# Key and value rows of the compression stored by offset within the stride, so that 66 moving elements lie in a row

## The chip, the cores and the metric

The kernel runs on one core of a Trainium2 chip. The metric is the device time of one execution in microseconds, as the median of several runs. The core has five engines with queues of their own: TensorE (PE in the profile, and PEld for its weight loads), VectorE (DVE), ScalarE (ACT), GpSimd (POOL) and SyncE (SP), which here only issues transfers.

## What is computed

Two transformer blocks over 512 tokens of width 1024, all in 32-bit floats. The change lies in the first block, in the compression of keys and values (`compress`): from the raw key (or value) rows of 512 tokens, 2 groups of 64 elements each, it takes overlapping windows of 32 tokens at a stride of 16, adds a position term, and sends each window of 32 x 64 = 2048 numbers through a small two-layer network.

```python
CMP_LEN, CMP_STRIDE, CMP_HIDDEN = 32, 16, 256

def compress(kv_raw, pos, w1, w2):
    B, T = kv_raw.shape[0], kv_raw.shape[1]
    nc = (T - CMP_LEN) // CMP_STRIDE + 1
    idx = jnp.arange(nc)[:, None] * CMP_STRIDE + jnp.arange(CMP_LEN)[None, :]
    blocks = kv_raw[:, idx] + pos[None, None, :, None, :]
    blocks = blocks.transpose(0, 1, 3, 2, 4).reshape(B, nc, N_KV_GROUPS, CMP_LEN * HEAD_DIM)
    return jax.nn.gelu(blocks @ w1) @ w2
...
    kc = rms_norm(compress(kv_heads(kcr), cmp_pos_k, cmp_w1_k, cmp_w2_k), k_cmp_norm_g)
    vc = compress(kv_heads(vcr), cmp_pos_v, cmp_w1_v, cmp_w2_v)
```

Everything else (the input projection, the three attention branches, the state-space mixer, and the whole second block) is the same before and after.

## The kernel before

Each engine runs one instruction stream that is written out by hand; the order on an engine is the order of the code, and semaphores (`S[...]`) tie the streams together. The 128 partitions hold a contraction index, the free axis holds tokens or columns. Large matrices are streamed from memory in "chunks" through a ring of two slots (`slot(c)`); SP issues the load of chunk c once TensorE has counted up `w_free` for the chunk two before it.

The part of the first block around the change runs on TensorE in this order.

1. Projections of the input: `proj_T` for the state-space input (4 tiles), then for the raw keys and the raw values (PT_KC and PT_KC + 1), each leaving a 128 x 512 result in a PSUM bank: partitions are 2 groups x 64 elements, columns are tokens. `proj_tok` follows for further keys and values (PT_KV, PT_KW). A projection tile may start once ScalarE has emptied the bank three or four tiles back (`proj_evac`).
2. ScalarE copies the raw keys (s = 0) and raw values (s = 1) into `x2`, a view of the buffer `xn_t` (lines 681 to 686). For each group g it writes the 512 tokens to the lower 64 partitions (line 684), and the same row moved by one token to the upper 64 partitions (line 685). So one column holds tokens t and t + 1, and one product contracts over two tokens x 64 elements = 128. GpSimd has zeroed the tail of each row before and put the position terms there as two extra windows (lines 522 to 526, counted by `zeroed`).
3. Transposes (L1122), the small products that build a Toeplitz kernel from the state-space weights (16 output columns), and the products behind `v_done`, 64 of them, each with 64 stationary columns and 64 moving elements.
4. The query projection, `proj_tok(PT_Q, ...)`.
5. **The compression's first layer**, lines 1152 to 1173. For s = 0, 1 (keys, values), for each half of the window (part), each half m of the 256 hidden units, each of 8 pairs of tokens lp, and each half h of 64 hidden units, one product: stationary 128 x 64 weights, moving 66 elements of `x2` (32 windows of group 0, 2 position columns, 32 windows of group 1). That is 2 x 2 x 2 x 8 x 2 = 128 products. The two products of h write the lower and the upper 64 partitions of one bank and read the same moving elements. The moving elements stand `CS` = 16 numbers, 64 bytes, apart:

```python
at_ = 2 * (KD * part + lp)
flat[:, at_:at_ + 65 * CS + 1:CS]
```

The key weights are chunk 6 (`ring`); the first half of the value weights lies in `arena` (`w1v_first`, loaded from ScalarE's queue at L717), the second half is chunk 7 (`w1v_last`), for which TensorE waits at s = 1, part = 1. After each s, TensorE counts `hid_done` and `w_free` up; the latter lets SP load chunk 8, then chunk 9 (the weights of the two gate projections).
6. The output of the state-space mixer, counted by `y_done`: 128 products with 64 stationary columns and 64 contiguous moving elements; again two neighbouring products fill the two halves of a bank and read the same moving elements (`toe_of(g)` and `cl3` against `u_in` and `st`).
7. `proj_T` for the gate projection (PT_ZS), with the compression's second layer inside its third tile; it needs `hid_gelu` from VectorE, which adds the positions and computes the gelu (L1893 to L1913) with ScalarE's tanh (L724) in between.

The later use of `xn_t` (line 731 on) is for other data.

Of the kernel before, what the change touches and what calls it, by code (L numbers as in the profile page):

```python
# [9 lines left out]
T = 512  # L10
D = 1024
P = 128
NT = T // P
KD = D // P
AW = 512
NH, HD, NG = 8, 64, 2
CL, CS, NCMP = 32, 16, 32
SG, SC, SN = 32, 16, 64
GP = SG // 2
LC = 8  # L20
NCH = T // LC
NAH, DAH, DAV = 8, 4, 128
GRID, GROWS = 64, 8
# [39 lines left out]
def build(nc, io):  # L63
# [3 lines left out]
    ACT = mybir.ActivationFunctionType  # L67
# [4 lines left out]
    with ctx:  # L72
# [9 lines left out]
        def cut(view, **dims):  # L82
            return view.rearrange("p (" + " ".join(dims) + ") -> p " + " ".join(dims), **dims)
# [7 lines left out]
        xn_t = sb("xn_t", 2 * NG * (T + 2 * CS))  # L91
# [46 lines left out]
        bank = [ctx.enter_context(nc.psum_tensor(f"bank{i}", [P, 512], fp32)) for i in range(8)]  # L138
# [4 lines left out]
        def col(name):  # L143
            return cols[:, COLS[name][0]:COLS[name][1]]
# [7 lines left out]
        x = cut(x_t[:, :], i=NT, f=D)  # L152
        hT = cut(hT_t[:, :], k=KD, t=T)
        xn = cut(xn_t[:, 0:2 * D], b=2, f=D)
        x2 = cut(xn_t[:, :], s=2, g=NG, t=T + 2 * CS)
        prob = cut(soft[:, 0:4 * T], b=4, t=T)
        probT = cut(soft[:, 4 * T:6 * T], b=2, t=T)
        ident = con("ident")
# [341 lines left out]
        @block.gpsimd  # L500
        def _(pool):
            steps = [0]

            def settle(ins):
                ins.then_inc(S["pool_step"], 1)
                steps[0] += 1
                pool.wait_ge(S["pool_step"], steps[0])

            def inv_root(mean, eps, done, of):

                settle(pool.tensor_scalar(of(ss), of(ss), 1.0 / mean, eps, MUL, ADD))
                pool.tensor_tensor(of(rstd), of(ss), of(mhalf), ALU.pow).then_inc(S[done], 1)

            def by_tile(v):
                return cut(v[:, 0:48], i=NT, h=12)

            settle(pool.memset(mhalf, -0.5))
            settle(pool.memset(gate_b[:, :], 0.0))
            pool.wait_ge(S["x_stats"], 1)
            inv_root(D, EPS, "x_rstd", lambda v: v[:, 0:NT])  # L520
            pool.wait_ge(S["xT_done"], 2 * NT)
            settle(pool.memset(x2[:, :, :, T - 1:T + 2 * CS], 0.0))

            pool.wait_ge(S["params_in"], 32)
            settle(pool.tensor_copy(x2[:, 0, 0, T:T + 2 * CS:2], col("pos_k")))
            pool.tensor_copy(x2[:, 1, 0, T:T + 2 * CS:2], col("pos_v")).then_inc(S["zeroed"], 1)
            pool.wait_ge(S["cl_ready"], 1)
            settle(pool.memset(soft[:, 0:2048], 0.0))
            pool.wait_ge(S["cl_ready"], 2)
            pool.memset(spent, 0.0).then_inc(S["zeroed"], 1)  # L530
            pool.wait_ge(S["k_stats"], 1)
            inv_root(HD, EPS, "k_rstd", lambda v: by_tile(v)[:, :, 8:12])
            for r in range(2):
                pool.wait_ge(S["q_stats"], r + 1)
                inv_root(HD, EPS, "q_rstd", lambda v: by_tile(v)[:, 2 * r:2 * r + 2, 0:8])
            pool.wait_ge(S["k_stats"], 2)
            inv_root(HD, EPS, "k_rstd", lambda v: v[0:NG * NCMP, 48:49])
            pool.wait_ge(S["proj_done"], PT_ZA + 4)
            for i in range(NT):
                pool.dma_start(x[:, i, :], io["x"].rearrange("(r c) f -> c r f", r=GROWS)[16 * i:16 * (i + 1)]).then_inc(S["x_back"], 16)  # L540

            pool.wait_ge(S["ssm_ready"], 4)
            for f in range(4, KD):
                settle(pool.tensor_copy(a_hi[:, f, :], hT[:, f, :]))
                pool.tensor_tensor(hT_r[:, f, :], hT[:, f, :], a_hi[:, f, :].bitcast(fp32), SUB).then_inc(S["ssm_lo"], 1)
            pool.wait_ge(arrive[CH_WO % SLOTS], landed(CH_WO))
            for j in range(4):
                pool.tensor_copy(wo_hi(j), wo_raw(0, j)).then_inc(S["wo_hi"], 1)
                pool.wait_ge(S["wo_hi"], j + 1)
                pool.tensor_tensor(wo_lo(0, j), wo_raw(0, j), wo_hi(j).bitcast(fp32), SUB).then_inc(S["wo_lo"], 1)  # L550

            def load_bias(n):
                l, h = divmod(n, LOADS)
                if n >= 2:
                    pool.wait_ge(*bias_read(n - 2))
                if h < DAH:
                    pool.dma_start(bias_ring[:, n % 2, 0:896], io["t5_bias"][h]).then_inc(bias_in[n % 2], 16)
                else:
                    src = io["na_bias"][l, 2 * (h - DAH):2 * (h - DAH) + 2].rearrange("h p j -> p h j")
                    pool.dma_start(cut(bias_ring[:, n % 2], h=2, j=1024), src).then_inc(bias_in[n % 2], 16)  # L560

            def x_rstd(r):

                sums = cut(ssq[:, 0:2 * NT], c=2, i=NT)
                for a in range(2):
                    pair = slice(2 * a, 2 * a + 2)
                    pool.wait_ge(S["n_stats"], 2 * r + a + 1)
                    settle(pool.tensor_tensor(ss[:, pair], sums[:, 0, pair], sums[:, 1, pair], ADD))
                    inv_root(D, EPS, "n_rstd", lambda v: v[:, pair])

            pool.wait_ge(S["x_ready"], 1)
            for l in range(LAYERS + 1):
                if l:
                    pool.wait_ge(S["xn_ready"], NT * (l + 1))
                pool.dma_start(gain, io["gains"][l]).then_inc(S["gain_in"], 16)
                x_rstd(l)
                if l == LAYERS:
                    break
                at_ = LOADS * l
                for n in range(at_ + (2 if l else 0), at_ + DAH + 2):  # L580
                    load_bias(n)
                pool.wait_ge(S["o_stats"], l + 1)
                inv_root(DAV, SUB_EPS, "o_rstd", lambda v: v[:, 0:NT * DAH])
                for n in range(at_ + DAH + 2, min(at_ + LOADS + 2, LOADS * LAYERS)):
                    load_bias(n)
# [3 lines left out]
        def _(act):  # L589
# [15 lines left out]
            for i in range(NT):  # L605

                ins = act.activation(xn[:, i % 2, :], x[:, i, :], ACT.Square, accum_out=ss[:, i:i + 1])
# [67 lines left out]
            for f in range(4):  # L675
                src = proj(PT_U + f)[:, :].rearrange("p (n s) -> p s n", s=LC)
# [4 lines left out]
            for s in range(2):  # L681
                src = proj(PT_KC + s)
                for g in range(NG):
                    act.activation(x2[0:HD, s, g, 0:T], src[g * HD:(g + 1) * HD, :], ACT.Copy)
                    ins = act.activation(x2[HD:P, s, g, 0:T - 1], src[g * HD:(g + 1) * HD, 1:T], ACT.Copy)
                ins.then_inc(S["proj_evac"], 1)
                part_hi(8 + s)
            part_hi(10)
# [6 lines left out]
            for i in range(NT):  # L695
                src = proj(PT_KV + i)
# [7 lines left out]
            for i in range(NT):  # L704
                src = proj(PT_KW + i)
# [12 lines left out]
            for i in range(NT):  # L718
                src = proj(PT_Q + i)
# [45 lines left out]
            for i in range(NT):  # L765
# [3 lines left out]
                if i == 0:  # L769
                    act.wait_ge(S["kc_T"], 1)  # L770
                    for u in range(2):
                        half_ = slice(u * HD, (u + 1) * HD)
                        ins = act.activation(kcT[half_, :, u, :], cut(bank[7][half_, 0:NG * NCMP], g=NG, j=NCMP), ACT.Copy)
# [167 lines left out]
            for l in range(LAYERS):  # L941
                for half in (1, 0):
                    for g in range(4 - 4 * half, 8 - 4 * half):
                        for t in range(4):
                            u = first_unit(l, g + 1)
# [52 lines left out]
        def _(pe):  # L998
# [3 lines left out]
            def mm(out, lhsT, rhs, first, last):  # L1002
                return pe.matmul(out, lhsT, rhs, start=first, stop=last)  # L1003
# [146 lines left out]
            w1k = slot(CH_W1, 16, 256)  # L1150
            w1v_last = slot(CH_W1 + 1, KD, 256)
            for s in range(2):
                flat = x2[:, s].rearrange("p g t -> p (g t)")
                for part in range(2):
                    if s and part == 0:
                        pe.wait_ge(S["w1v_in"], 16)
                    elif part == s:
                        arrived(CH_W1 + s)
                    w = (w1v_last if part else w1v_first) if s else w1k[:, KD * part:KD * (part + 1)]
                    for m in range(2):  # L1160
                        if s == 0 and part == 0:
                            pe.wait_ge(S["proj_evac"], PT_Q + 3 + m)
                        for lp in range(KD):
                            at_ = 2 * (KD * part + lp)
                            for h in range(2):
                                c = m * P + h * SN
                                ins = mm(bank[m][h * SN:(h + 1) * SN, s * 66:(s + 1) * 66], w[:, lp, c:c + SN], flat[:, at_:at_ + 65 * CS + 1:CS],
                                         part == 0 and lp == 0, part == 1 and lp == KD - 1)
                ins.then_inc(S["hid_done"], 1)
                pe.wait_ge(S["hid_done"], s + 1)  # L1170
                pe.sem_inc(S["w_free"], 1)
# [82 lines left out]
            w = slot(CH_GLU, 4, 512)  # L1254
# [1097 lines left out]
```

## Time and profile before

| | us |
|---|---|
| Time before, median of 3 runs | 973.33 (971.76 to 974.12) |
| The profiled execution's own time | 974.55 |
| its span, first to last instruction | 972.7 |
| TensorE busy in it | 925.0 (95%) |
| VectorE busy | 579.5 (60%) |
| ScalarE busy | 453.5 (47%) |
| GpSimd busy | 66.6 (7%) |

The span is what the trace covers; the profiled execution's time holds 1.85 us more, outside of it. "took" or "mean ns of one" is the time from start to modelled end of one instruction. Matmuls overlap, so the price of one in a dense row is the distance from start to start, and not what it took. A 32-bit product stands in the trace as two matmul records and two weight-load records: the 128 products of the compression are 256 records of each kind. "issue" is time in which an engine waited for nothing that the profile shows.

### The profile page before, as it was taken

The numbers are of one execution on the slowest core, as the hardware profiler recorded it, in microseconds if no ns is written. First come the engines' busy times: TensorE is split into PE (matmuls) and PEld (weight loads), VectorE is DVE, ScalarE is ACT, GpSimd is POOL, SyncE is SP. The second block draws the span as 40 slices with busy tenths as digits, with TensorE's granted clock in tenths as the row PEclk, the third lists the DMA queues.
The fourth block names the chain that finished last, engine by engine and source line by source line (L and its number), as shares of the span: only waits on it lengthen the run. The fifth ranks groups of instructions, "written<-read, shape, count | busy, mean of one in ns | idle before, by whom it ended". The sixth has DMA issues, their size and how long they took to land.

```text
span 972.7 us, 14853 instructions
## 1 busy us (share of the span) xinstructions
PE 925.0 (95%) x5845; PEld 725.6 (75%) x5845; DVE 579.5 (60%) x1177; ACT 453.5 (47%) x974; POOL 66.6 (7%) x82
## 2 busy tenths in 40 slices
PE   3999999999999999999999989999999999998995
PEld 1689897764667788886788867888886778886784
DVE  5899867977886472438762347254244964435632
ACT  4635124455785343336824248233423853426730
POOL 1001120004400010000010000000000010000000
PEclk9999999999999999998999999999999899998999
DMA  9845654265100333432304323132443123323102
GB/s 357 311 115 130 149 174 140 98 174 193 68 2 3 106 125 87 119 98 62 107 25 127 108 89 105 42 93 80 111 131 103 45 84 108 87 94 102 66 1 87
DMA packets 94807, 104.71 MB, mean 108 GB/s; under 512 B 15953, under 2 KB 65105, under 8 KB 94738
## 3 DMA queue, kind: packets, MB, share of 16 engines
q1 hardware_dynamic: 89586, 86.62, 29.1%
q0 software_dynamic: 3824, 15.73, 5.1%
q10 hardware_dynamic: 1328, 1.41, 0.5%
q8 instruction: 47, 0.77, 0.3%
q14 instruction: 22, 0.18, 0.1%
HBM read 98.37 MB, written 4.19 MB: 105 GB/s over the span
## 4 chain that ended last, share of the span: by engine, by line
PE 83%; DVE 6%; ACT 5%; issue 3%; DMA 3%; DVEq 0%; SPq 0%; POOL 0%; POOLq 0%; ACTq 0%; PEldq 0%
PE bank L1003 77%; DVE ring L2016 2%; PE bank L1332 2%; ACT ring L913 2%; DMA ring<-in_w_in 2%; PE bank L1312 1%; DMA ring<-in_w_ada 1%; PE bank L1470 1%; ACT soft L920 1%; PE bank L1388 1%; ACT w_hi L863 0%; PE bank L1378 0%; ACT hT_hi L845 0%; DVE small L1596 0%; ACT arena L710 0%
## 5 line engine op out<-in xcount | busy, mean ns | idle before, releaser
L2071 DVE TENSOR_TENSOR w_lo<-ring,w_hi 128x1024 fp32r<-128x1024 f32 x80 | 97.7, 1225 | 114.7 <-ACT w_hi L863 111.9
L1003 PE MATMUL bank<-w_hi,hT_hi 128*128 128x512 f32 x320 | 125.3, 392 | 1.3 <-issue 1.0
L1003 PE MATMUL bank<-hT_hi,w_hi 128*128 128x512 f32 x320 | 125.7, 393 | 0.0
L1003 PE MATMUL bank<-w_lo,hT_hi 128*128 128x512 f32 x320 | 124.6, 389 | 0.0
L1003 PE MATMUL bank<-hT_lo,w_hi 128*128 128x512 f32 x320 | 124.6, 389 | 0.0
L1003 PE MATMUL bank<-w_hi,hT_lo 128*128 128x512 f32 x320 | 124.6, 389 | 0.0
L1003 PE MATMUL bank<-hT_hi,w_lo 128*128 128x512 f32 x320 | 124.5, 389 | 0.0
L863 ACT ACTIVATE w_hi<-ring 128x1024 fp32r<-128x1024 f32 x80 | 84.4, 1058 | 11.7 <-PE bank L1003 11.4
L1003 PEld LDWEIGHTS bank<-w_hi,hT_hi 128*128 128x128 f32 x320 | 60.1, 188 | 14.8 <-issue 2.6
L1003 PEld LDWEIGHTS bank<-hT_hi,w_hi 128*128 128x128 f32 x320 | 60.1, 188 | 13.1 <-issue 0.7
L1003 PEld LDWEIGHTS bank<-hT_lo,w_hi 128*128 128x128 f32 x320 | 60.1, 188 | 12.7
L1003 PEld LDWEIGHTS bank<-w_lo,hT_hi 128*128 128x128 f32 x320 | 60.1, 188 | 12.6
L1003 PEld LDWEIGHTS bank<-w_hi,hT_lo 128*128 128x128 f32 x320 | 60.1, 188 | 12.2
L1003 PEld LDWEIGHTS bank<-hT_hi,w_lo 128*128 128x128 f32 x320 | 60.1, 188 | 12.0
L868 ACT ACTIVATE bank<-x_t 128x512 f32<-128x512 f32 x24 | 14.5, 602 | 96.7 <-DVE x_t L2267 63.4
L1003 PE MATMUL bank<-arena 128*64 128x64 f32 (+5 forms) x608 | 51.0, 293 | 2.1 <-issue 1.7
L815 ACT ACTIVATE ring<-ring,small 128x512 f32<-128x512 f32 x64 | 45.7, 715 | 15.5 <-DVE small L2016 12.7
L2203 DVE SCALAR_TENSOR_TENSOR k_lo<-bank,k_hi 128x512 fp32r<-128x512 f32 x16 | 11.1, 692 | 53.2 <-ACT k_hi L933 53.2
L1003 PEld LDWEIGHTS bank<-arena 128*64 128x64 f32 (+1 forms) x608 | 31.1, 147 | 14.4 <-issue 12.6
L2016 DVE CUSTOM_DVE_ANT_0 ring<-bank,bias_ring 128x512 f32<-128x512 f32 x64 | 41.4, 684 | 0.0
L913 ACT ACTIVATE ring<-ring,small 128x256 f32<-128x256 f32 x64 | 31.9, 499 | 14.4 <-DVE small L2149 14.2
L2267 DVE TENSOR_TENSOR x_t<-bank,x_t 128x512 f32<-128x512 f32 x16 | 11.0, 689 | 45.9 <-PE bank L1003 45.9
(312 smaller groups left out, 1811.1 us busy)
## 6 DMA issues: line engine op xcount, KB each, us to landing
ring<-in_w_in SPq DMA_DIRECT2D x66, 512.0 KB, 4.5
ring<-in_w_ada SPq DMA_DIRECT2D x4, 2048.0 KB, 14.1
ring<-in_w_in SPq DMA_DIRECT2D x4, 2048.0 KB, 8.9
bias_ring<-in_na_bias POOLq DMA_DIRECT2D x8, 1024.0 KB, 5.6
ring<-in_w_out SPq DMA_DIRECT2D x16, 512.0 KB, 3.4
ring<-in_w_out SPq DMA_DIRECT2D x2, 2048.0 KB, 8.1
bias_ring<-in_t_bias POOLq DMA_DIRECT2D x8, 448.0 KB, 3.7
x_t<-in_x SPq DMA_DIRECT2D x4, 512.0 KB, 5.8
```

The lines of the kernel that those rows point to most:

```text
L815: act.activation(p, p, ACT.Exp, scale=-1.0, bias=negm[:, k % 8:k % 8 + 1], accum_out=ssum[:, k % 8:k % 8 + 1])\
L863: act.activation(w_hi[:, u % 4], raw_w[:, u % 4], ACT.Copy).then_inc(S["w_hi_ready"], 1)
L868: settle(act.activation(place[:, 0:n], x[:, i, c0:c0 + n], ACT.Square, accum_out=ssq[:, part * NT + i:part * NT + i + 1]))
L913: act.activation(p, p, ACT.Exp, scale=-1.0, bias=negm[:, k % 16:k % 16 + 1], accum_out=ssum[:, k % 16:k % 16 + 1])\
L920: act.activation(probT2[:, m % 4, :], bank[m % 2][:, :], ACT.Copy).then_inc(S["na_moved"], 1)
L1003: return pe.matmul(out, lhsT, rhs, start=first, stop=last)
L1312: ins = pe.transpose(bank[u % 2][:, b * P:(b + 1) * P], src[:, b * P:(b + 1) * P], ident)
L1332: ins = pe.transpose(bank[k % 2][:, b * P:(b + 1) * P], prob1_of(k)[:, b * P:(b + 1) * P], ident)
L2016: dve.tensor_tensor_reduce(prob_of(k)[:, 0:width], bank[S_BANKS[k % 4]][:, 0:width], bias, -scale, 3.0e38, ADD, MIN, negm[:, k % 8:k % 8 + ...
L2071: dve.tensor_tensor(w_lo[:, u % 4], raw_w[:, u % 4], w_hi[:, u % 4].bitcast(fp32), SUB).then_inc(S["w_split"], 1)
L2203: dve.scalar_tensor_tensor(lo_[:, t, :], bank[(pt2(l, g) + t) % 4][:, :], SCALE if isq else 1.0, hi_[:, t, :].bitcast(fp32), MUL, SUB).the ...
L2267: dve.tensor_tensor(xs, bank[6 + t % 2][:, :], xs, ADD).then_inc(S["x_ready"], 1)
```

## The change

The buffer `xn_t` is read through another view, `win_x`, with the axes s (keys, values), r (8), g (2), j (34). Token t = 16 j + 2 r + u of group g stands in the partitions of half u at (r, g, j): r and u are the token's offset within the stride of 16, j is the stride that it lies in. j = 32 and 33 hold the zeros and the position columns that stood behind the tokens before.

```diff
-        x2 = cut(xn_t[:, :], s=2, g=NG, t=T + 2 * CS)
+        win_x = cut(xn_t[:, 0:2 * 8 * NG * WIN], s=2, r=8, g=NG, j=WIN)
...
-            settle(pool.memset(x2[:, :, :, T - 1:T + 2 * CS], 0.0))
+            for s in range(2):
+                settle(pool.memset(win_x[:, s, :, :, NCMP:WIN], 0.0))
 
             pool.wait_ge(S["params_in"], 32)
-            settle(pool.tensor_copy(x2[:, 0, 0, T:T + 2 * CS:2], col("pos_k")))
-            pool.tensor_copy(x2[:, 1, 0, T:T + 2 * CS:2], col("pos_v")).then_inc(S["zeroed"], 1)
+            pos_at = [win_x[:, s, :, 0, NCMP:WIN].rearrange("p r j -> p j r") for s in range(2)]
+            settle(pool.tensor_copy(pos_at[0], cut(col("pos_k"), j=2, r=8)))
+            pool.tensor_copy(pos_at[1], cut(col("pos_v"), j=2, r=8)).then_inc(S["zeroed"], 1)
...
                 for g in range(NG):
-                    act.activation(x2[0:HD, s, g, 0:T], src[g * HD:(g + 1) * HD, :], ACT.Copy)
-                    ins = act.activation(x2[HD:P, s, g, 0:T - 1], src[g * HD:(g + 1) * HD, 1:T], ACT.Copy)
+                    pairs = src[g * HD:(g + 1) * HD, :].rearrange("p (j r u) -> p u r j", j=NCMP, r=8, u=2)
+                    for u in range(2):
+                        ins = act.activation(win_x[u * HD:(u + 1) * HD, s, :, g, 0:NCMP], pairs[:, u], ACT.Copy)
...
-                flat = x2[:, s].rearrange("p g t -> p (g t)")
+                wins = win_x[:, s].rearrange("p r g j -> p r (g j)")
...
-                            at_ = 2 * (KD * part + lp)
...
-                                ins = mm(bank[m][h * SN:(h + 1) * SN, s * 66:(s + 1) * 66], w[:, lp, c:c + SN], flat[:, at_:at_ + 65 * CS + 1:CS],
+                                ins = mm(bank[m][h * SN:(h + 1) * SN, s * 66:(s + 1) * 66], w[:, lp, c:c + SN], wins[:, lp, part:part + 66],
```

With `WIN = NCMP + 2` = 34. A product for the second half of the window (part = 1) reads the same row r, one element further on. ScalarE reads its bank in steps of 16 numbers and writes 8 rows of 32 numbers, and it writes each token once, to the half of its parity, where before it wrote each token to both halves. GpSimd zeroes 2 x 32 numbers per partition in two instructions, for 132 in one.

No instruction changes its place on any engine; TensorE, VectorE and SyncE have the same instructions in the same order. What differs is the form of twelve instructions on ScalarE and GpSimd. ScalarE, after the projections of the state-space input, before:

```order
L663 ACTIVATE a_hi<-ring 128x1024
L684 ACTIVATE xn_t<-bank 64x512
L685 ACTIVATE xn_t<-bank 64x511
L684 ACTIVATE xn_t<-bank 64x512
L685 ACTIVATE xn_t<-bank 64x511
L663 ACTIVATE a_hi<-ring 128x560
```

and after the change (lines are 3 or 4 further down), the same stretch with the second group, for the values:

```order
L666 ACTIVATE a_hi<-ring 128x1024
L689 ACTIVATE xn_t<-bank 64x8x32 x4
L666 ACTIVATE a_hi<-ring 128x560
L689 ACTIVATE xn_t<-bank 64x8x32 x4
L666 ACTIVATE a_hi<-ring 128x560 x2
```

The eight copies stand where they stood, and each moves 256 numbers per partition in place of 512 or 511.

## Rows read from the trace of the kernel before

**Rows 1.** The page: the chain that ended last, shares by engine and line.
```profile
PE 83%; DVE 6%; ACT 5%; issue 3%; DMA 3%; DVEq 0%; SPq 0%; POOL 0%; POOLq 0%; ACTq 0%; PEldq 0%
```
**Rows 2.** The chain, 126 to 176 us: start us, us, what.
```profile
126.41 7.72 PE bank L1003 x128
134.13 0.14 issue
134.27 7.68 PE bank L1003 x128
141.96 0.29 issue
142.24 6.17 PE bank L1003 x204
148.41 1.72 issue
150.13 25.25 PE bank L1003 x168
```
**Rows 3.** Timeline of TensorE: start us, us, engine, line, operation, out<-in, shapes, count.
```profile
99.88 3.95 PE L1003 MATMUL bank<-arena 128*64 128x64 f32 x128
...
142.38 0.32 PE L1003 MATMUL bank<-arena 128*64 128x64 f32 x4
...
148.10 0.32 PE L1003 MATMUL bank<-arena,gate_b 128*64 128x64 f32 x4
```
**Rows 4.** Groups by line and shape: count | busy us, mean ns | idle before.
```profile
L1003 PE MATMUL bank<-xn_t,ring 128*64 128x66 f32 x192 | 11.6, 295 | 0.3 <-PE bank L1003 0.3
L1003 PE MATMUL bank<-arena,soft 128*64 128x64 f32 x64 | 3.8, 223 | 0.3 <-PE bank L1003 0.3
```
**Rows 5.** Windows: stretch, us, busy (records) of PE, PEld, DVE, ACT, POOL; clock, DMA, GB/s.
```profile
126.40:142.00 15.60, 15.38 (x256) 14.92 (x256) 8.59 (x8) 1.83 (x3) 7.24 (x4) 1.00 0.63 204
142.20:148.40 6.20, 6.16 (x204) 6.06 (x204) 5.68 (x17) 2.31 (x3) 0.00 (x0) 1.00 0.89 300
```
**Rows 6.** Timeline of SyncE, and the issues by line: KB each, us to landing.
```profile
126.23 0.39 SPq L453 DMA_DIRECT2D ring<-in_cmp_w_v  x1
134.24 0.37 SPq L453 DMA_DIRECT2D ring<-in_w_in  x1
...
ring<-in_w_in SPq DMA_DIRECT2D x2, 2048.0 KB, 8.9
...
ring<-in_cmp_w_v SPq DMA_DIRECT2D x1, 1024.0 KB, 5.8
ring<-in_glu_w SPq DMA_DIRECT2D x1, 1024.0 KB, 8.0
```
**Rows 7.** Timeline of VectorE around the end of the compression.
```profile
134.12 1.22 DVE L1810 TENSOR_REDUCE small<-soft 128x16 f32<-128x1024 f32 x1
142.05 0.16 DVE L1893 COPY small<-bank 128x2 f32<-128x2 f32 x1 [6.71 <-PE bank L1003]
...
147.68 2.36 DVE L1620 TENSOR_TENSOR ring_lo<-ring,a_hi 128x1024 fp32r<-128x1024 f32 x2
```
**Rows 8.** Timeline of ScalarE: an emptied bank read in steps of 8, the copies, the tanh.
```profile
58.11 0.60 ACT L677 ACTIVATE arena<-bank 128x512 f32<-128x512 f32 x1 [4.04 <-PE bank L1003]
...
69.83 0.59 ACT L684 ACTIVATE xn_t<-bank 64x512 f32<-64x512 f32 x1 [2.42 <-PE bank L1003]
...
144.72 0.42 ACT L724 ACTIVATE pw<-pw 128x256 f32<-128x256 f32 x1 [16.46 <-DVE pw L1903]
145.04 1.99 ACT L663 ACTIVATE a_hi<-ring 128x1024 fp32r<-128x1024 f32 x2
```
**Rows 9.** The page: records of PE and PEld, and the instruction queue's packets and MB.
```profile
PE 925.0 (95%) x5845; PEld 725.6 (75%) x5845; DVE 579.5 (60%) x1177; ACT 453.5 (47%) x974; POOL 66.6 (7%) x82
...
q8 instruction: 47, 0.77, 0.3%
```
**Rows 10.** Timeline of TensorE in the token projection behind the raw values.
```profile
69.63 0.28 PE L1003 MATMUL bank<-a_hi,x_hi 128*128 128x256 f32 x1
69.87 0.28 PE L1003 MATMUL bank<-ring_lo,x_hi 128*128 128x256 f32 x1
69.98 0.28 PE L1003 MATMUL bank<-a_hi,x_hi 128*128 128x256 f32 x1
```
**Rows 11.** Timeline of GpSimd, the last of the instructions that the change touches there.
```profile
26.65 0.66 POOL L526 COPY xn_t<-cols 128x16 f32<-128x16 f32 x1
```

More of the change, by code:

```diff
@@ L20 @@
 LC = 8
+WIN = NCMP + 2
 NCH = T // LC
```

## The prediction, made before the changed kernel ran

> **What bounds the kernel now.** I read the shares of the chain of waits first: TensorE holds 83% of it [rows 1], so what counts is time on TensorE's own stream, and time saved on another engine counts only where TensorE waits for it. Then I read the chain in the stretch of the change. From 126.41 to 141.96 us it is nothing but the compression's 256 matmul records, two pieces of 7.72 and 7.68 us, and behind them the mixer's output in two pieces with a hole of 1.72 us between, and the gate projection [rows 2]. No other engine stands in it. So the compression is on the path with its full length, 7.72 + 7.68 = 15.40 us.
>
> Then the price of one record. 15.40 us / 256 = **60.2 ns** from start to start for 66 moving elements. The same kind of record with 64 contiguous moving elements is to be had twice. In the mixer's output, fours of records start 142.38 ... 148.10 us, 49 fours apart, so 5.72 / 196 = **29.2 ns**; in the products behind `v_done` it is 3.95 us for 128, at most 30.9 ns with the tail of the last one in it [rows 3]. Shapes, weights (64 stationary columns), the change of halves within a bank and the granted clock (1.00, the 2.4 GHz level, in both stretches [rows 5]) are the same. Neither is it only the distance: a record took 295 ns in the compression and 223 ns in the mixer's output [rows 4], 72 ns more, so each streams for longer. The weight loads follow the matmuls in both (256 and 204 of each [rows 5]), and they run at 29.2 ns there, so they are not what holds the compression at 60. What is left is the one thing that differs: 66 elements 64 bytes apart against 64 in a row, at twice the price.
>
> No row shows 66 contiguous elements, or strided ones elsewhere. The Trainium skill (SBUF — State Buffer, section Specifications (TRN2)) says that SBUF is read in lines of 16 bytes and that each step to a new line pays a penalty; it gives no amount. By it, and this is an estimate from the page's figure, every one of the 66 reads pays now, and about one in four would after.
>
> **The change, part by part.**
>
> *The 128 products.* Contiguous, a record should cost 29.2 x 66/64 = 30.1 ns, the whole 256 x 30.1 = 7.71 us, so **15.40 - 7.71 = 7.7 us less**. By the other stretch's 30.9 ns it is 256 x 31.9 = 8.2 us, so 7.2 us less. I take 7.7, since 30.9 holds a tail. The other bound is that the stride was innocent: 0.
>
> *ScalarE's eight copies.* They are 0.59 us each now [rows 8]. A bank read in steps of 8 numbers took 0.60 for 512 elements [rows 8], the same as these contiguous ones, so steps cost ScalarE nothing there; with 256 elements each is between 0.3 (half) and 0.6 us. Nobody waits for them: the values' copies begin at 69.83 us and the first reader of their semaphore on TensorE is the fourth token tile of the next projection. The records there start 0.117 us apart (69.63, two later 69.87, 69.98) [rows 10], 12 per tile, so the fourth starts 36 x 0.117 = 4.2 us behind 69.63, at 73.8; the copies end at 72.3 now. Saved time there is idle time: 0.
>
> *GpSimd.* One more small instruction; the last of these ends at 27.3 us [rows 11], and ScalarE asks for it at 64.3. Hidden by 37 us: 0. At the next bound, 0.66 us each as the dearest copy, still 0.
>
> *What follows the compression earlier.* Four things have to be there 7.7 us sooner, or 3.9 us for those halfway.
> First `w1v_last`: issued at 126.23, 5.8 us to landing [rows 6], so there at 132.0. It is wanted after three quarters of the compression: 138.03 now, then 126.41 + 0.75 x 7.71 + 0.14 = **132.3**. It just fits, with 0.3 us to spare. Another load of the same size took 8.0 us [rows 6]; by that it lands at 134.2 and TensorE waits 1.9 us. I take 0, since 5.8 is this load's own time and nothing else is queued ahead of it, and keep 1.9 for the range.
> Second the gate weights: issued when s = 0 is done, 134.24 now, then 126.41 + 3.86 + 0.1 = 130.4; 8.9 us to landing [rows 6] is 139.3. ScalarE's split follows the tanh, 144.72 now [rows 8]. VectorE sits idle for 6.71 us before the compression's end and is done with its squares at 134.12 + 1.22 = 135.34 [rows 7]; with the compression done at 134.3 it can start at 135.4 in place of 142.05, 6.65 us earlier and no more. So tanh at 138.1, split of the first tile at 139.3 to 140.4, and VectorE's low parts, whose pair ends at 147.68 + 2.36 = 150.04 now [rows 7], at 143.4 to 143.5. TensorE wants the gate projection's first tile at 151.8 - 7.7 = 144.1. All three fit, the closest by 0.6 us.
> Third `hid_gelu`, wanted 17 us into the gate projection: far. Fourth SP's own queue: it waits for TensorE's counts and comes earlier with them.
>
> *The hole of 1.72 us.* It is put down to "issue": TensorE waited for nothing that the profile shows, in the middle of one run of products [rows 2]. The candidate is the supply of instructions. Queue 8 moved 47 packets, 0.77 MB, 16.4 KB each, and 5845 + 5845 records / 47 is 249 per packet [rows 9]: this is TensorE's program, loaded while it runs. The compression's 512 records took 15.5 us, 7.7 us for each packet's worth; the mixer's first 408 took 6.2 us, 3.7 us for each, while the data transfers were busy at 0.89 [rows 5], and then came the hole. After the change the dense run is 1024 records at 3.7 us for each packet's worth. One hole, shifted, stays in my sum at 1.72 us, unchanged: the `v_done` stretch ran dense for 3.95 us without any, and the first dense packet's worth was free there. Bounds: none at all (1.7 us gained), or one for each of the four packets' worth, 4 x 1.72 = 6.9, 5.2 us more than now.
>
> *Sum.* 7.7 + 0 + 0 + 0 + 0 = 7.7 us off the profiled execution's 974.55, so 966.9. That execution lay 1.2 us above the median of the runs shown, 973.33; on the median, **965.6 us**. Behind this stretch TensorE's work is tied to TensorE's own progress (loads, copies and weights are released by its counts), so I expect nothing given back.
>
> **The rivals.**
>
> *A, more holes.* The doubled pace starves TensorE's program twice or more. For it: the hole exists, it came after about 400 dense records, and now there are 1024 with big loads under most of them. Against: the loads of data before 142 were less dense (0.63 [rows 5]). Price 1.72 us each: two holes 967.4, three 969.1, four 970.8. A wait for `w1v_last` of 1.9 us looks the same in the sum (967.5).
>
> *B, the hole vanishes,* because the loads fall elsewhere: 965.6 - 1.7 = 963.9.
>
> *C, the stride was innocent.* The 60.2 ns come from something that the change keeps (accumulation 16 deep, the weights' place, decoding), and it doesn't do what it says: 973.3. Against: the same pairs of halves at 29.2 ns [rows 3], and the 72 ns longer records [rows 4]. The Trainium skill (TensorE: Matmul & The Clock Gate, section Wait — 56ns, not 53.3ns?) has a figure for it: without hardware decode the sequencer spends about 62 ns on each matmul whatever its size. By that rule 60.2 would be the floor, and the time stays 973.3. The 29.2 ns in the same program speak against it.
>
> *D, slower.* ScalarE pays for reading PSUM in steps of 16 numbers. Its place is the proj_evac wait at 73.8 us. With X per copy, eight copies and a split of 0.67 us between end at 64.3 + 8X + 0.7, so TensorE waits for X over 1.1 us, it eats the whole gain at X = (7.7 + 8.8)/8 = 2.1 us, and at 2.5 us the loss is 11.2, the time 973.3 - 7.7 + 11.2 = 976.8. For it: no row has steps of 16. Against: steps of 8 cost nothing, and it would take seven times the half of 0.59.
>
> **How the numbers follow.** Forecast 0.56 (965.6, own range 964.5 to 966.7 by the bounds 7.2 and run-to-run spread); A 0.19 (967 to 971); B 0.12; C 0.10; D 0.03. Runs of before spread over 2.4 us, about 1.2 each way. The range takes in the forecast, B with 0.9 us of spread below it, and A up to two holes and part of a wait, 969.5; left out are C, D and A's tail, some 0.17. A difference of 0.3%, 2.9 us, is about what a measurement can tell from none. Faster: forecast, B and nearly all of A, 0.86. Same: C and A's far end, 0.11. Slower: D, 0.03.
>
> **What would show it.** In the profile after, the records with 66 moving elements 30 ns apart, 7.7 us in all; their mean "took" near 225 ns; the copies at 0.3 to 0.6 us with no wait of TensorE behind them; the mixer's output starting at 134.4; the "issue" pieces between 126 and 145 us, one of about 1.7. The forecast is wrong if records stay at 60 ns (C), if "issue" pieces add up to over 3 us (A), if a wait on `ring<-in_cmp_w_v` stands at 132 us, or if a later stage ends as late as before, with TensorE waiting for VectorE at the gate projection.

## The result, and the profile after

The changed kernel takes **967.12 us** (median of 7 runs, 966.37 to 970.27) against 973.17 us for the kernel before (7 runs, 971.76 to 974.12); the ratio is 0.9948, with a 95% interval of 0.9933 to 0.9964. In a second comparison it was 967.98 us (5 runs) against 972.81 us, ratio 0.9955 (0.9943 to 0.9968). The medians lie 6.1 and 4.8 us apart, the ratios stand for 5.1 and 4.4, so the gain is about 5 us, where 7.7 were forecast. The profiled execution took 967.12 us with a span of 965.2.

The chain of waits through the stretch (start us, us, what), which answers to [rows 2]:

```profile
127.16 3.97 PE bank L1007 x128
131.13 0.14 issue
131.27 2.46 PE bank L1007 x77
133.73 0.53 issue
134.25 1.75 PE bank L1007 x51
136.00 0.29 issue
136.29 2.44 PE bank L1007 x76
138.73 1.61 issue
140.34 3.95 PE bank L1007 x128
144.29 1.97 issue
146.26 25.26 PE bank L1007 x168
```

The compression's 256 records are busy for 3.97 + 2.46 + 1.75 = 8.18 us, where it was 15.40. But three holes (pieces of "issue" in the middle of like products; the short ones of 0.14 and 0.29 stood there before too) of 0.53, 1.61 and 1.97 us, 4.11 in sum, stand where one of 1.72 stood. The groups by line and shape show the records themselves shorter, 223 ns for 295 in [rows 4], and equal to those of the mixer's output:

```profile
L1007 PE MATMUL bank<-arena 128*64 128x64 f32 x320 | 13.8, 223 | 3.6 <-issue 3.6
...
L1007 PE MATMUL bank<-xn_t,ring 128*64 128x66 f32 x192 | 6.3, 223 | 0.8 <-issue 0.5 <-PE bank L1007 0.3
```

ScalarE's copies and GpSimd's instructions in the timeline, against [rows 8] and [rows 11]:

```profile
26.05 0.83 POOL L528 COPY xn_t<-cols 128x16 f32<-128x16 f32 x1
26.94 0.21 POOL L529 COPY xn_t<-cols 128x16 f32<-128x16 f32 x1
...
70.57 1.56 ACT L689 ACTIVATE xn_t<-bank 64x256 f32<-64x256 f32 x4 [3.25 <-PE bank L1007]
```

Four copies take 1.56 us, 0.39 each, for 0.59 before. The tanh of [rows 8], with as many elements in a row, took 0.42, so steps of 16 numbers in the bank cost nothing that shows. GpSimd is done at 27.15.

**The two profiles differ by more than the change.** From the compression's first record to the gate projection's first (timeline of TensorE, L1007) it is 147.93 - 127.16 = 20.77 us after and 151.80 - 126.41 = 25.39 before: 4.6 us less. The spans differ by 7.5. The rest lies in stretches that the change doesn't touch: the compression began 0.75 us later after the change, and what follows the gate projection's first record took 3.6 us less, with another granted clock. Windows of before (stretch, us, busy of PE, PEld, DVE, ACT, POOL, clock, DMA, GB/s):

```profile
576.00:592.00 16.00, 12.96 (x126) 9.46 (x126) 8.61 (x40) 11.43 (x35) 0.78 (x1) 0.89 0.29 100
882.00:895.00 13.00, 10.55 (x86) 7.60 (x84) 6.50 (x28) 7.85 (x24) 0.78 (x1) 0.74 0.37 123
151.80:972.70 820.90, 793.57 (x4561) 617.56 (x4557) 456.29 (x993) 393.66 (x877) 49.94 (x63) 0.98 0.29 89
```

and of after, the same work 4 to 6 us earlier:

```profile
572.00:588.00 16.00, 12.96 (x139) 9.53 (x137) 9.87 (x43) 12.73 (x39) 1.50 (x2) 1.00 0.30 103
877.00:889.00 12.00, 9.02 (x100) 6.82 (x102) 7.65 (x34) 9.34 (x28) 0.78 (x1) 1.00 0.41 133
147.93:965.20 817.27, 790.11 (x4561) 615.70 (x4557) 456.34 (x993) 393.47 (x877) 49.92 (x63) 0.99 0.29 90
```

Means of 0.89 and 0.74 say that before was at the 1.2 GHz level for a part of both stretches, and after, with 1.00, was not. TensorE waited there in both kernels, 0.4 to 1.4 us at a time. From the gate projection to the end it is 820.9 us against 817.3 for the same 4561 matmuls. This difference doesn't go with the change: in a second profile of the changed kernel the same work takes 820.6.

```profile
147.83:968.40 820.57, 793.77 (x4559) 618.12 (x4557) 456.32 (x993) 393.62 (x877) 49.95 (x63) 0.98 0.29 89
147.00:150.50 3.50, 3.50 (x28) 2.86 (x25) 2.24 (x7) 2.06 (x4) 0.00 (x0) 0.53 0.02 5
```

But one part of it may. The second line shows a fall to the 1.2 GHz level that neither kernel had in its first profile: it begins 1.2 us behind the third hole, and the piece of 168 records that starts at 145.90 took 26.78 us for 25.26. Whether the holes brought it on is not shown; the first profile, and the kernel with the reads alone changed (below), had three holes and no such fall.

So I compare the stretch from here on, and medians of several runs, and not spans.

### The profile page after: what moved, and what is told of

Its sections match the earlier page's. It is cut to its first block, busy times and chain, and to the rows that moved or that the text cites. A ratio compares the mean times of both kernels' runs of the same rounds, so it can differ in the third digit from the quotient of the medians.

```text
span 965.2 us, 14854 instructions
## 1 busy us (share of the span) xinstructions
PE 915.9 (95%) x5845; PEld 716.7 (74%) x5845; DVE 579.6 (60%) x1177; ACT 451.9 (47%) x974; POOL 66.8 (7%) x83
## 4 chain that ended last, share of the span: by engine, by line
PE 82%; DVE 6%; ACT 5%; issue 3%; DMA 2%; SPq 2%; DVEq 0%; POOL 0%; POOLq 0%; ACTq 0%
PE bank L1007 77%; DVE ring L2019 2%; PE bank L1335 2%; ACT ring L917 2%; DMA arena<-in_w_ada 2%; PE bank L1315 1%; PE bank L1473 1%; ACT soft L924 1%; PE bank L1391 1%; SPq L458 1%; SPq L456 1%; ACT w_hi L867 0%; PE bank L1381 0%; DVE small L1599 0%; ACT hT_hi L849 0%
## 5 line engine op out<-in xcount | busy, mean ns | idle before, releaser
L1007 PE MATMUL bank<-w_hi,hT_hi 128*128 128x512 f32 x320 | 125.3, 392 | 1.3 <-issue 1.0
L1007 PE MATMUL bank<-hT_hi,w_hi 128*128 128x512 f32 x320 | 125.7, 393 | 0.0
L1007 PE MATMUL bank<-w_lo,hT_hi 128*128 128x512 f32 x320 | 124.6, 389 | 0.0
L1007 PE MATMUL bank<-hT_lo,w_hi 128*128 128x512 f32 x320 | 124.6, 389 | 0.0
L1007 PE MATMUL bank<-hT_hi,w_lo 128*128 128x512 f32 x320 | 124.5, 389 | 0.0
L1007 PE MATMUL bank<-w_hi,hT_lo 128*128 128x512 f32 x320 | 124.5, 389 | 0.0
L1007 PEld LDWEIGHTS bank<-w_hi,hT_hi 128*128 128x128 f32 x320 | 60.1, 188 | 14.8 <-issue 2.6
L1007 PEld LDWEIGHTS bank<-hT_hi,w_hi 128*128 128x128 f32 x320 | 60.1, 188 | 13.1 <-issue 0.7
L1007 PEld LDWEIGHTS bank<-hT_lo,w_hi 128*128 128x128 f32 x320 | 60.1, 188 | 12.7
L1007 PEld LDWEIGHTS bank<-w_lo,hT_hi 128*128 128x128 f32 x320 | 60.1, 188 | 12.6
L1007 PEld LDWEIGHTS bank<-w_hi,hT_lo 128*128 128x128 f32 x320 | 60.1, 188 | 12.2
L1007 PEld LDWEIGHTS bank<-hT_hi,w_lo 128*128 128x128 f32 x320 | 60.1, 188 | 12.0
L1007 PE MATMUL bank<-arena 128*64 128x64 f32 (+5 forms) x608 | 51.1, 293 | 3.9 <-issue 3.6
L1007 PEld LDWEIGHTS bank<-arena 128*64 128x64 f32 (+1 forms) x608 | 30.6, 147 | 16.4 <-issue 14.5
L1007 PE MATMUL bank<-k_hi,q_hi 64*128 64x256 f32 (+1 forms) x128 | 31.5, 452 | 7.3 <-DVE k_lo L2206 3.9
```

## Experiments

Each kernel starts from the changed one unless said otherwise. "The stretch" is the time from the compression's first record to the gate projection's first.

### The changed kernel again

> The changed kernel, run anew beside the kernel before, to have its time and its holes on this chip. The profile after the change has 30 ns per record of the compression (7.8 us with the tails taken off) and three holes that no engine explains: 0.53, 1.61 and 1.97 us, against one of 1.72 before. Theory S (the supply of TensorE's program sets the holes): the holes stand at the same places in the program, 254 to 256 records apart (127 or 128 matmuls and as many weight loads), sum 3.5 to 4.5 us. Theory L (they are chance): other places, other sizes. Time: 0.9930 to 0.9965 of the kernel before, 4 to 6 us less.

Measured: 967.98 us, ratio 0.9955 (0.9943 to 0.9968), and in the chain:

```profile
133.53 0.64 issue
...
138.64 1.34 issue
...
143.93 1.97 issue
```

The holes stand behind the same records, the 205th, the 332nd and the 460th of the compression and the mixer's output together, and of nearly the same size. They are no chance. The stretch is 147.83 - 126.96 = 20.9 us. The hole of the kernel before also stands behind the 256 + 204 = 460th [rows 2]. Between two holes lie 127 or 128 matmuls and as many weight loads, 254 to 256 records: about one packet of queue 8, by [rows 9].

### What the distance of the elements costs

```diff
+                    step = (1, 2, 4, 8)[2 * s + part]
...
-                                ins = mm(bank[m][h * SN:(h + 1) * SN, s * 66:(s + 1) * 66], w[:, lp, c:c + SN], wins[:, lp, part:part + 66],
+                                ins = mm(bank[m][h * SN:(h + 1) * SN, s * 66:(s + 1) * 66], w[:, lp, c:c + SN], spread[:, lp + part:lp + part + 65 * step + 1:step],
```

`spread` is the buffer `xn_t` taken flat. A second kernel has the steps 3, 16, 5 and 31.

> The changed kernel, but the moving elements of the compression are read 1, 2, 4 and 8 numbers apart (4, 8, 16, 32 bytes) in its four quarters of 64 records each (keys first half, keys second half, values first half, values second half), from whatever stands in the buffer; the compressed keys and values are therefore others. Theory of lines (the price comes with each new 16-byte line that a read touches): 1 and 2 apart cost 30 ns per record, 4 and 8 apart 60 ns. Theory of any gap: 30 ns for 1 alone and 60 ns for 2, 4 and 8. Theory that the distance is innocent: all four at the same price. A mean took of about 223 ns goes with 30 ns and 295 ns with 60.

> As with steps 1, 2, 4 and 8 (30, 30, 62 and 62 ns per record), now 3, 16, 5 and 31 numbers apart in the four quarters. Theory of lines with a price for each new 16-byte line: 3 apart opens a new line at three reads of four, against one of two at 2 apart, which was free, so 1.5 times 30 = 45 ns; 5, 16 and 31 open one at each read, 60 ns, and more distance costs no more. Rival (the step counts, not the lines: everything past 8 bytes costs double): 3 apart is 60 ns too.

Measured, timeline of TensorE for steps 1 and 2 (one row), 4, 8:

```profile
127.05 4.04 PE L1007 MATMUL bank<-xn_t,ring 128*64 128x66 f32 x128 [0.30 <-PE bank L1007]
131.24 4.05 PE L1007 MATMUL bank<-xn_t,arena 128*64 128x66 f32 x64 [0.15 <-PE bank L1007]
135.07 4.13 PE L1007 MATMUL bank<-xn_t,ring 128*64 128x66 f32 x64
```

and for steps 3 and 16 (one row), 5, 31:

```profile
126.36 6.87 PE L1007 MATMUL bank<-xn_t,ring 128*64 128x66 f32 x128 [0.30 <-PE bank L1007]
133.38 4.09 PE L1007 MATMUL bank<-xn_t,arena 128*64 128x66 f32 x64
137.26 4.07 PE L1007 MATMUL bank<-xn_t,ring 128*64 128x66 f32 x64
```

128 records at steps 1 and 2 take 4.04 us, against 3.97 at step 1 alone: 31 to 32 ns each, with the tail of the last in it. 64 records at step 4 take 4.05, at 5 4.09, at 8 4.13, at 31 4.07 us, 63 to 65 ns each; in the kernel before, at step 16, such a quarter took 3.96 and 3.92. From the first record of the third quarter to the first of the fourth, so without the tail, it is in the changed kernel

```profile
131.27 2.09 PE L1007 MATMUL bank<-xn_t,arena 128*64 128x66 f32 x64
133.15 0.57 PE L1007 MATMUL bank<-xn_t,ring 128*64 128x66 f32 x13
```

1.88 us at step 1, and by the rows above 3.83 at step 4, 3.88 at step 5, and at step 16 in the kernel before 138.03 - 134.27 = 3.76: 29.4, 59.8, 60.6 and 58.8 ns per record. Step 3 has 6.87 - 3.85 = 3.0 us for 64, 47 ns (3.85 is 15.40 / 4). Nearly free at 2, one and a half times at 3, twice from 4 on and no more at 31: that goes with the number of new 16-byte lines per element (1/4, 1/2, 3/4, 1), free up to one half. The rule of the Trainium skill (SBUF — State Buffer, section Specifications (TRN2)), that a line wants two hits for full bandwidth, agrees: with two elements per line (step 2) the 128 records cost 0.07 us more than with four, with one per line (step 4) a record costs 59.8 ns for 29.4.

Both kernels have one hole only, of 1.78 and 2.15 us, and it stands behind the 460th record again. Where the compression runs slower, the first two holes are absent.

### Reads alone, and storage alone

The kernel before with its own storage and copies, reading in a row (`flat[:, at_:at_ + 66]`):

> The kernel before, with its storage and its copies, but each product of the compression reads 66 numbers in a row, which are then other tokens; the compressed keys and values are others. If the reads alone are the gain: 30 ns per record as after the change, and the same holes as after it (some 0.5, 1.5 and 2 us). If the new storage or the shorter copies had a part in it: dearer than 30 ns per record.

The changed kernel with its storage and copies, reading 16 apart (`spread[:, 2 * lp + part:2 * lp + part + 65 * CS + 1:CS]`):

> The changed kernel with its storage and its copies, but the products read 16 numbers apart again; the compressed keys and values are others. If the reads alone are the gain: 60 ns per record, 15.4 us for the compression, and one hole of 1.7 to 2 us in the mixer's output, as in the kernel before. The rival (storage has a part): below 60 ns.

Measured, the chain of the first:

```profile
126.85 3.97 PE bank L1003 x128
...
133.41 0.49 issue
...
138.37 1.61 issue
...
143.94 1.70 issue
```

and of the second:

```profile
126.36 7.61 PE bank L1007 x128
...
134.10 7.65 PE bank L1007 x128
...
148.21 1.44 issue
```

Reading in a row brings the whole change, its three holes (0.49, 1.61, 1.70) with it, and a stretch of 147.30 - 126.85 = 20.5 us; the new storage without it leaves the compression at 7.61 + 7.65 = 15.26 us, for 15.40, and one hole, of 1.44 where 1.7 to 2 had been expected. Single executions took 966.48 and 970.53 us, beside 971.10 for the kernel before. Copies, zeroes and layout have no part in the time beyond 0.14 us.

### Is a hole a matter of what is moved meanwhile?

The load of the second gate projection's weights is held back until the mixer's output is done:

```diff
                 if c >= SLOTS:
                     sp.wait_ge(S["w_free"], c - SLOTS + 1)
+                if c == CH_ZA:
+                    sp.wait_ge(S["y_done"], 4)
```

> The changed kernel, but the load of the second gate projection's weights (2 MB) is issued only once the mixer's output is done, about 8 us later. Nothing in the computation changes. Theory S1 (TensorE's program packets come late because the big data loads are ahead of them in the transfer engines): the third hole, 1.97 us, which lies under this load, shrinks below 0.5 us; the first two (0.53 and 1.61), under the first gate projection's load, stay; the time is 2 us below the changed kernel, about 965. Theory S2 (a packet takes its 6 us whatever else is moved; only the density of the program counts): three holes stay with 4 us in sum and the time is that of the changed kernel, 967. Rival W: the late load is itself waited for at the second gate projection; then TensorE waits there and the time is above the changed kernel's.

> The kernel before, with the same late load of the second gate projection's weights. There the only hole is 1.72 us in the mixer's output, under that load. Theory S1: the hole is gone or below 0.4 us, the span 1.7 us shorter than before's. Theory S2: it stays at 1.5 to 2.0 us. The compression stays at 60.2 ns per record.

Measured: 966.07 us, ratio 0.9927 (0.9912 to 0.9942), 1.9 us under the changed kernel in the same comparison; in a second comparison 966.63 us, ratio 0.9927 (0.9915 to 0.9938), with holes of 0.46 and 1.61. The chain of the first:

```profile
133.19 0.92 issue
...
138.58 1.34 issue
139.92 29.00 PE bank L1009 x296
```

The third hole is gone, and the mixer's output runs into the gate projection without a break; the first two stay. The stretch is 145.32 - 126.63 = 18.7 us. In the kernel before with the same edit, a single execution, the only hole is gone too, and the stretch is 150.15 - 126.70 = 23.5 us for 25.4 (969.23 us; that is more below 972.81 than the hole was long, and its mean clock was 0.994, where those runs of the kernel before had 0.985 to 0.990):

```profile
142.53 31.20 PE bank L1005 x372
```

Where the packet comes late can be seen in the transfers of the changed kernel (packets, MB, and queue 8's own). TensorE took up a new packet's worth at 134.25 us, and the next packet, the only one of queue 8 up to 140.4, moved between 137.5 and 138.5:

```profile
DMA packets 197, 0.39 MB, mean 391 GB/s; under 512 B 13, under 2 KB 13, under 8 KB 196
...
q8 instruction: 1, 0.02, 6.9%
```

With the late load a packet's worth was taken up at 139.92, and the next packet moved between 140.5 and 141.5, alone:

```profile
DMA packets 1, 0.02 MB, mean 16 GB/s; under 512 B 0, under 2 KB 0, under 8 KB 0
...
q8 instruction: 1, 0.02, 7.5%
```

In narrower windows the two fall in 137.9 to 138.0 and 141.0 to 141.1. So it is 3.7 us to the transfer under the load, and 1.1 us on idle transfer engines. From the packet to TensorE's next record it is then 140.34 - 137.9 = 2.4 us, and so it is at every hole: in the twelve profiles that have one, 20 holes in all, a packet of queue 8 moved 2.3 to 2.7 us before TensorE went on. That ties the holes to the packets. It also gives the sum: a dense packet's worth is used up in 3.95 us, 1.1 + 2.4 = 3.5 us fits within it, and 3.7 + 2.4 = 6.1 us does not. The whole round under load, from one resumption to the next, is 140.34 - 134.25 = 6.1 and 146.26 - 140.34 = 5.9 us.

### The same with the other load

Of the first gate projection's weights, an eighth is loaded (`[:, 0:1]` of the eight blocks), beside the late second load; the rest is left out, so the kernel computes something else:

> The kernel with the late second load, and of the first gate projection's weights only an eighth is loaded (256 KB for 2 MB; the rest of the weights is stale, so that projection's result is another). Theory S1: with the 2 MB load gone from under the compression's second half and the mixer's output, the hole of 1.34 us goes to below 0.3 us; the first hole (0.92 us in the last run), whose packet comes while the last value weights land, shrinks or stays below 1. Theory S2 (only density): both stay, 2.2 us in sum. The mixer's output should end 1.3 to 2.2 us earlier than with the late load alone.

Measured, the chain (span 961.2 us, one execution):

```profile
133.73 0.57 issue
...
136.34 15.79 PE bank L1010 x290
```

With that load cut to 256 KB the second hole is gone as well. The first, 0.57 us, stays; the packet for it is due while the last of the value weights comes in.

### A version from it: the first gate projection's weights in two loads

The weights are needed, so only their time can move. The first 128 (or 256) of 512 columns are loaded where the whole was, the others after the mixer's output, beside the late second load:

```diff
                 for n, ((k, w, a, b), src) in enumerate(parts):
+                    if c == CH_ZS and n:
+                        sp.wait_ge(S["y_done"], 4)
```

> The kernel with the late load of the second gate projection's weights, and the first gate projection's weights in two loads: 128 of 512 columns (512 KB) where the whole load was issued, the other 384 (1.5 MB) once the mixer's output is done. Theory S1: the second hole (1.34 us with the late load alone) falls below 0.5 us, since the 512 KB are landed before its packet is asked for; the first (0.6 to 0.9) stays; the mixer's output ends 1 us sooner. Rival W: the second tile of the gate projection now waits for the rest of its weights; they are issued at 142 and need some 8 us, the tile is due at about 148, so up to 3 us are lost there. If both hold, the sum is 0 to 2 us above the late load alone (966); if only S1, it is 1 us below.

> As with the split at 128, but 256 columns (1 MB) come first, so the first two tiles need nothing late, and the third is due 11 us behind the end of the mixer's output. Theory S1: 1 MB lands at about 137; the second hole, whose packet is asked for at 134, shrinks from 1.34 to between 0.3 and 1.0 us, and no tile waits. Time 0.3 to 1 us below the late load alone, ratio to the kernel before 0.991 to 0.993. Theory S2: the hole stays at 1.3.

> The late load of the second gate projection's weights alone, for comparison on the same chip: the third hole away, the first two there (2.0 to 2.4 us in sum), ratio to the kernel before 0.991 to 0.994, as in its first run (0.9927).

Measured: split at 128, 967.5 us, ratio 0.9940 (0.9929 to 0.9952); split at 256, **964.09 us, ratio 0.9902 (0.9889 to 0.9915)**. Both lose the second hole and keep a first one of 0.37 us; for 256 a second one of 0.3 to 1.0 us and a ratio of 0.991 to 0.993 had been expected, so it came out better. The stretch is 16.6 us in both. At 128 the second tile waits for its weights; the waits of TensorE:

```profile
PE bank L1016 <- ACT a_hi L675: 2.1, 1, 2.1
PE bank L1016 <- DVE ring_lo L1632: 1.0, 1, 1.0
```

ScalarE's split comes 2.1 us late and VectorE's part 1.0 more. At 256 nothing waits, and the chain is

```profile
134.09 0.37 issue
...
136.50 31.20 PE bank L1016 x372
```

with one hole of 0.37 us left. That beats both kernels, and is the fastest here that computes the whole. It lies 2.5 us below the late load alone, and the stretches account for 1.9 of that.

It also shows what a packet does not wait for. TensorE took up a packet's worth at 134.46 us, and the packet moved between 135.8 and 135.9, 1.3 us later, though the transfer engines were as busy as in the changed kernel. What moved in between here (134.46 to 135.8) and there (134.25 to 137.9):

```profile
DMA packets 501, 0.51 MB, mean 382 GB/s; under 512 B 1, under 2 KB 501, under 8 KB 501
...
DMA packets 717, 1.47 MB, mean 402 GB/s; under 512 B 0, under 2 KB 0, under 8 KB 717
```

The rates are alike, the amounts are not. So the wait goes with how much of a load is still to come when the packet is asked for, and not with the rate; by which rule the two share the transfer engines is not shown.

| kernel | stretch, us | holes in it, us | ratio to before |
|---|---|---|---|
| before | 25.4 | 1.72 | 1 |
| changed | 20.8, 20.9 | 0.53 + 1.61 + 1.97, 0.64 + 1.34 + 1.97 | 0.9948, 0.9955 |
| and second load late | 18.7, 18.5 | 0.92 + 1.34, 0.46 + 1.61 | 0.9927, 0.9927 |
| and first load split at 128 | 16.6 | 0.37 | 0.9940 |
| and first load split at 256 | 16.6 | 0.37 | 0.9902 |

## Why the prediction was right, and where it was not

*The time.* 967.12 lies in the range of 963.0 to 969.5, and it is faster as forecast, but the forecast proper, 965.6 with its own range to 966.7, was missed. What happened is rival A, with three holes that sum to less than three of its price; it had 967.4 for two and 969.1 for three. The range held it because it had been drawn to take in most of A; the mechanism that carried most of the chance, one hole as before, is not what happened. And that the profiled execution, at 967.12, lies so near to the 966.9 reckoned for it is luck: of the 7.4 us between the two profiled executions only 4.6 lie in the stretch.

*What bounds it.* Right: the stretch stood on the chain with its full length, and what it lost was not given back later. The same 4561 matmuls behind it took 817.3 and 820.6 us, for 820.9 before.

*The 128 products.* The mechanism was right, and nothing but the reads did it. The term was a little mis-sized. In the half that no hole breaks it is 131.27 - 127.16 = 4.11 us for 134.27 - 126.41 = 7.86 [rows 2], 3.75 less, so 7.5 for both halves, where 7.7 were taken. The cause is the division 15.40 / 256: its quotient of 60.2 ns holds the tails of two pieces, which the change does not shorten (from start to start it is 58.8), while the 29.2 ns had been read without them. The busy pieces differ by 15.40 - 8.18 = 7.2; that this is the lower bound of the prediction is chance, since 0.3 of it comes from the first hole, which splits a piece and adds a tail.

*Copies, GpSimd.* Zero, as said. The copies are 0.39 us, within the 0.3 to 0.6.

*What follows earlier.* Right. `w1v_last` took 5.4 us to landing and was not waited for. VectorE began at 136.10 in place of 142.05, right behind its squares (135.4 had been reckoned), and ScalarE had the gate weights at 140.2, for 139.3 forecast; no engine was waited for at the gate projection.

*The hole.* This is the step of the forecast that failed. "One hole, shifted, stays in my sum" was argued from the `v_done` stretch, that ran dense for 3.95 us without any. That is one packet's worth, and it was no evidence for four in a row. The other number stood in the same paragraph: before the change the hole had come in the second dense packet's worth, and four were to follow each other. The holes are 4.11 us for 1.72, 2.4 us lost, and the two holes more split a row each and add a tail, 0.27 and 0.22 us from start to start. With 7.5 - 2.4 - 0.5 = 4.6 the stretch's gain of 4.6 us is accounted for. The cause named there, the supply of TensorE's program, is as far as these runs can tell the right one: a packet precedes the end of each hole by the same 2.3 to 2.7 us. Density is only a half of it: in the kernel before and in the changed one, holes go when the big load is moved away at the same density, and the first two are absent, with the same loads issued, when the compression runs slower (storage alone, and the kernels with steps up to 8 and up to 31). The price of 1.72 us was good for the second and third hole (1.61, 1.97), and too high for the first (0.53).

*What stays open.* The first hole, 0.37 to 0.92 us in eight profiles, falls just after the last value weights have landed (1 MB); its packet moved at 131.7 us, while they came in. By the same reasoning that load should be its cause. A kernel that moves it was not made, so it is argued and not shown. Nor is it shown how the packets are fetched, only when they move, and what the 2.4 us between a packet and the next record are spent on.

*Slower, and the stride innocent* (rivals D and C) are both refuted, D by the copies' 0.39 us and C by the records 29.4 ns apart, with the reads alone changed.

## What to carry to other kernels

Look at the step of the moving operand before its count: read in a row or at a distance of two 32-bit numbers, a record of 66 elements cost 30 ns here, at four and more 60, and a copy that has to be made anyway can lay the data out for it at no cost. When a stretch of small products doubles its pace, count its records in packets of the program, and look what is being loaded beneath it: the program comes through the same transfer engines, and holding back one large load and half of another until they are needed brought about as much again as the change itself (ratio 0.9902 for 0.9948 and 0.9955). Held back too far, a load is waited for, and most of that is gone again (0.9940 with the split at 128). A hole under "issue" in one run of like instructions is where to look.

## What had not been expected of the hardware

- A step of 3 numbers costs one and a half times (3.0 us for 64 records, against 3.85 at 16 and about 2.0 at 1), so the price grows with the lines opened and is not a switch; step 3 is the only point between.
- With 2 MB loads moving at some 390 GB/s, TensorE's supply was one packet of 16.4 KB in 5.9 to 6.1 us; the same packet on idle transfer engines moved 1.1 us after one was taken up, and no hole came. Nor did one come when only 0.51 MB moved first, at 382 GB/s.
- TensorE went on 2.3 to 2.7 us after a packet had moved, at every one of 20 holes.
- The same program, profiled twice, took 817.3 and 820.6 us for the same work behind the stretch, with a mean granted clock of 0.99 and 0.98: two profiles of one kernel can differ by nearly as much as this change brings.
